# An expert's down product moved into the step of its gate and up products, with down's weights stored in one piece per partition

## The reference

```python
for gi in range(MOE_GROUPS):
    hg = jnp.einsum('td,edf->tef', t, w_gate[gi])
    hu = jnp.einsum('td,edf->tef', t, w_up[gi])
    act = jax.nn.silu(hg) * hu * gates[:, gi, :, None].astype(t.dtype)
    out = out + jnp.einsum('tef,efd->td', act, w_down[gi])
return out.reshape(b, s, d)
```

## Time and profile before

| | |
|---|---|
| median of 3 runs | 887.52 us (885.52 to 888.07) |
| the profiled execution | 885.81 us |
| its span on the core | 883.7 us |
| TensorE busy | 778.8 us, 88% |
| VectorE, ScalarE busy | 219.8 and 138.6 us |
| mean granted clock of TensorE | 0.954 of full |
| DMA | 245.29 MB, 278 GB/s over the span |

### The profile page before, as it was taken

The page is one execution under the profiler, slowest core; times in us unless marked ns, Lnnn a source line. Parts: engine busy times, 40 slices in busy tenths (PEclk is TensorE's granted clock), DMA queues, the critical chain, the costliest instruction groups (busy, mean ns, idle before and its releaser), DMA issues.

```text
span 883.7 us, 7888 instructions
## 1 busy us (share of the span) xinstructions
PE 778.8 (88%) x3080; PEld 350.3 (40%) x3080; DVE 219.8 (25%) x596; ACT 138.6 (16%) x337; POOL 29.9 (3%) x49
## 2 busy tenths in 40 slices
PE   4999977958999899989999968858999989898996
PEld 2455553553333333333445534455333323232342
DVE  0212332162124121112221452251313312121222
ACT  2013210312111010100211132122111111110031
POOL 5000000000000000000000020000000000000000
PEclk9999997969999999999999978969999999999999
DMA  8982226523999999999994070270999999999601
GB/s 249 369 299 96 95 96 263 213 94 142 383 428 418 422 423 420 421 420 406 360 199 164 0 309 1 82 299 12 365 418 424 423 418 423 418 425 415 242 1 47
DMA packets 47590, 245.29 MB, mean 278 GB/s; under 512 B 2496, under 2 KB 4768, under 8 KB 39360
## 3 DMA queue, kind: packets, MB, share of 16 engines
q1 hardware_dynamic: 45088, 240.66, 69.2%
q0 software_dynamic: 1104, 2.45, 1.0%
q10 hardware_dynamic: 1360, 1.66, 0.7%
HBM read 243.70 MB, written 1.06 MB: 277 GB/s over the span
## 4 chain that ended last, share of the span: by engine, by line
PE 67%; DMA 21%; DVE 5%; issue 4%; ACT 1%; SPq 1%; POOL 0%; ACTq 0%; POOLq 0%; DVEq 0%
DMA weights<-in_moe_w_up_dram 20%; PE bank L696 17%; PE bank L489 15%; PE bank L501 10%; PE bank L709 8%; PE bank L717 4%; PE bank L684 2%; PE bank L647 1%; PE bank L803 1%; PE bank L476 1%; PE bank L703 1%; DMA residual<-in_x_dram 1%; PE bank L537 1%; PE bank L870 1%; PE bank L861 1%
## 5 line engine op out<-in xcount | busy, mean ns | idle before, releaser
L696 PE MATMUL bank<-weights,expert_rows 128*64 128x512 f32 x1024 | 234.6, 612 | 35.1 <-DMA weights<-in_moe_w_up_dram 28.8
L696 PEld LDWEIGHTS bank<-weights,expert_rows 128*64 128x64 f32 x1024 | 84.6, 140 | 180.0 <-issue 180.0
L489 PE MATMUL bank<-weights,normalised 128*128 128x512 f32 (+1 forms) x352 | 149.9, 583 | 3.0 <-issue 3.0
L709 PE MATMUL bank<-weights,hidden_turned 128*64 128x512 f32 x512 | 116.9, 598 | 1.2 <-DVE hidden_turned L1455 0.6
L489 PEld LDWEIGHTS bank<-weights,normalised 128*128 128x128 f32 x352 | 67.1, 194 | 78.8 <-issue 77.9
L501 PE MATMUL bank<-weights,normalised 128*128 128x512 f32 x192 | 85.8, 606 | 5.6 <-ACT normalised L944 5.6
L1455 DVE COPY hidden_turned<-bank 128x256 f32<-128x256 f32 x32 | 13.6, 425 | 294.2 <-PE bank L703 294.2
L717 PE MATMUL bank<-expert_outputs,scatter_onehots 64*128 64x512 f32 x256 | 63.6, 615 | 2.4 <-ACT expert_outputs L948 2.4
L709 PEld LDWEIGHTS bank<-weights,hidden_turned 128*64 128x64 f32 x512 | 34.3, 136 | 78.8 <-issue 78.8
L501 PEld LDWEIGHTS bank<-weights,normalised 128*128 128x128 f32 x192 | 36.9, 194 | 51.5 <-issue 51.4
L1070 ACT ACTIVATE gate_tanh<-bank 128x256 f32<-128x256 f32 x32 | 12.3, 383 | 243.3 <-PE bank L696 243.3
(11 more groups left out here) (226 smaller groups left out, 507.9 us busy)
## 6 DMA issues: line engine op xcount, KB each, us to landing
weights<-in_moe_w_gate_dram SPq DMA_DIRECT2D x32, 2048.0 KB, 21.7
weights<-in_moe_w_up_dram SPq DMA_DIRECT2D x32, 2048.0 KB, 26.5
weights<-in_moe_w_down_dram SPq DMA_DIRECT2D x32, 2048.0 KB, 19.5
weights<-in_even_w_in_dram SPq DMA_DIRECT2D x6, 2048.0 KB, 17.1
weights<-in_ple_w_gate_dram SPq DMA_DIRECT2D x4, 2048.0 KB, 28.1
weights<-in_even_w_out_dram SPq DMA_DIRECT2D x2, 2048.0 KB, 18.4
weights<-in_odd_w_qkv_dram SPq DMA_DIRECT2D x2, 2048.0 KB, 19.5
weights<-in_odd_w_out_dram SPq DMA_DIRECT2D x4, 1024.0 KB, 21.5
```

The source lines that it names most:

```text
L489: mm = pe.matmul(B[bank][:, 0:width], XT[:, k, tok(t)], w[:, k, :], start=(k == 0), stop=(k == KD - 1))
L696: mm = pe.matmul(bank[j * BLK:(j + 1) * BLK, :].rearrange("p (m f) -> p m f", m=2), rows[:, k, :], W[:, slot:slot + 2, a:a + FF // 2], sta ...
L709: mm = pe.matmul(B[7][half * BLK:(half + 1) * BLK, :], ACTT[:, 2 * (f % 2) + f // 2, :], wd[:, f, half * 512:(half + 1) * 512], start=(f = ...
```

## The change

Step e of TensorE becomes: gate and up of expert e, the scatter of e-1, the transposes of e, down of e. There are 16 steps and not 17, and a down slot comes free in the step of its own gate and up. VectorE copies the turned hidden values ahead of the onehots, and ScalarE copies down's product in the same step. Down is loaded as gate and up are, rows 4p to 4p+3 in one run of 16 KB for each partition. For this each half j of the array gets other hidden columns: of every four neighbouring columns it takes two (4q+2j and 4q+2j+1), so the streamed operand of `gate_up` is read in pairs of floats, 16 bytes from pair to pair; and `turned_back` reads every second float of `US`. The counts of instructions of every kind stay as they are.

```diff
             def load(srcs, e, m, dst, done):

                 s = srcs[m][e]
-                if m < 2:
-                    sp.dma_start(dst, s.rearrange("(p k) f -> p (k f)", p=P)).then_inc(done, 16)
-                else:
-                    sp.dma_start(dst.rearrange("p (k d) -> p k d", k=KF), s.rearrange("(k p) d -> p k d", p=P))\
-                        .then_inc(done, 16)
+                sp.dma_start(dst, s.rearrange("(p k) n -> p (k n)", p=P)).then_inc(done, 16)
...
                     for k in range(KD):
                         for j in range(2):
-                            a = k * FF + j * (FF // 2)
-                            mm = pe.matmul(bank[j * BLK:(j + 1) * BLK, :].rearrange("p (m f) -> p m f", m=2), rows[:, k, :],
-                                           W[:, slot:slot + 2, a:a + FF // 2], start=(k == 0), stop=(k == KD - 1))
+                            w = W[:, slot:slot + 2, k * FF:(k + 1) * FF].rearrange("p m (q j c) -> p m q j c", j=2, c=2)
+                            mm = pe.matmul(bank[j * BLK:(j + 1) * BLK, :].rearrange("p (m q c) -> p m q c", m=2, c=2),
+                                           rows[:, k, :], w[:, :, :, j, :], start=(k == 0), stop=(k == KD - 1))
...
                     for c in range(2):
-                        mm = pe.transpose(B[6][:, c * P:(c + 1) * P], US[:, c * P:(c + 1) * P], ident)
+                        mm = pe.transpose(B[6][:, c * P:(c + 1) * P], US[:, c:2 * P:2], ident)
...
+                    gate_up(B[4 + e % 2], XE[:, e % 2], n % NSLOT).then_inc(sem("gate_up_ready"), 1)
                     if e >= 1:
-                        pe.wait_ge(sem("act_ready"), v())
-                        if v() >= 2:
-                            pe.wait_ge(sem("actt_ready"), v(-1))
-                        if e in (4, 6):
-                            pe.wait_ge(sem("pT_copied"), 2 * l + e // 2 - 1)
-                        turned_back().then_inc(sem("act_turned"), 1)
-                    if e >= 2:
-                        pe.wait_ge(sem("pt2_ready"), v(-1))
-                        pe.wait_ge(sem("ys_ready"), v(-1))
-                        scatter(e % 2, e == 2, 0)
-                        scatter(e % 2, e == 2, 1).then_inc(sem("sc_done"), 1)
-                    if e >= 1:
-                        wait_unit(u0 + 3 * (e - 1) + 2)
+                        pe.wait_ge(sem("pt2_ready"), v())
+                        pe.wait_ge(sem("ys_ready"), v())
+                        scatter((e - 1) % 2, e == 1, 0)
+                        scatter((e - 1) % 2, e == 1, 1).then_inc(sem("sc_done"), 1)
+                    pe.wait_ge(sem("act_ready"), v(1))
+                    if v() >= 1:
                         pe.wait_ge(sem("actt_ready"), v())
-                        if v() >= 2:
-                            pe.wait_ge(sem("ys_ready"), v(-1))
-                        down(unit(u0 + 3 * (e - 1) + 2).rearrange("p (k d) -> p k d", k=KF)).then_inc(sem("y_ready"), 1)
+                    if e in (4, 6):
+                        pe.wait_ge(sem("pT_copied"), 2 * l + e // 2 - 1)
+                    turned_back().then_inc(sem("act_turned"), 1)
+                    wait_unit(u0 + 3 * e + 2)
+                    pe.wait_ge(sem("actt_ready"), v(1))
+                    if v() >= 1:
+                        pe.wait_ge(sem("ys_ready"), v())
+                    down(unit(u0 + 3 * e + 2).rearrange("p (k d) -> p k d", k=KF)).then_inc(sem("y_ready"), 1)
...
-                for e in range(NE + 1):
+                for e in range(NE):
                     step(e)
```

More of the change, by code:

```diff
@@ L744, in step @@
[L744 to L754 removed]
+                    pe.wait_ge(sem("xe_ready"), v(1))
@@ L1065, in step @@
                     v = NE * l + e
-                    if e < NE:
-                        act.wait_ge(sem("gate_up_ready"), v + 1)
-                        if v >= 1:
-                            act.wait_ge(sem("ag_ready"), v)
-                        act.activation(TH, B[4 + e % 2][:, 0:256], ACT.Tanh, scale=0.5).then_inc(sem("th_ready"), 1)
+                    act.wait_ge(sem("gate_up_ready"), v + 1)
+                    if v >= 1:
+                        act.wait_ge(sem("ag_ready"), v)
+                    act.activation(TH, B[4 + e % 2][:, 0:256], ACT.Tanh, scale=0.5).then_inc(sem("th_ready"), 1)
                     if e < NE - 2:
                         rows(e + 2)
-                    if 1 <= e <= NE:
-                        act.wait_ge(sem("y_ready"), v)
-                        if e >= 3:
-                            act.wait_ge(sem("sc_done"), (NE - 1) * l + e - 2)
-                        copy(YS[:, (e - 1) % 2, :], B[7][:, :]).then_inc(sem("ys_ready"), 1)
-                for e in range(NE + 1):
+                    act.wait_ge(sem("y_ready"), v + 1)
+                    if e >= 2:
+                        act.wait_ge(sem("sc_done"), (NE - 1) * l + e - 1)
+                    copy(YS[:, e % 2, :], B[7][:, :]).then_inc(sem("ys_ready"), 1)
+                for e in range(NE):
                     step(e)
@@ L1471, in step @@
                     v = NE * l + e
-                    if 1 <= e <= NE:
-                        dve.wait_ge(sem("act_turned"), v)
-                        if v >= 2:
-                            dve.wait_ge(sem("y_ready"), v - 1)
-                        hidden_turned(sem("actt_ready"))
-                    if e < NE:
-                        gu = B[4 + e % 2]
-                        dve.wait_ge(sem("th_ready"), v + 1)
-                        dve.scalar_tensor_tensor(out=AG, in0=TH, scalar=1.0, in1=gu[:, 0:256], op0=ALU.add, op1=ALU.mult)\
-                            .then_inc(sem("ag_ready"), 1)
-                        dve.wait_ge(sem("ag_ready"), v + 1)
-                        dve.tensor_tensor(US, AG, gu[:, 256:512], ALU.mult).then_inc(sem("act_ready"), 1)
-                        if e >= 2:
-                            dve.wait_ge(sem("sc_done"), (NE - 1) * l + e - 1)
-                        onehots(e % 2, OC[:, e:e + 1], sem("first_onehots"), v + 1, sem("pt2_ready"))
+                    gu = B[4 + e % 2]
+                    dve.wait_ge(sem("th_ready"), v + 1)
+                    dve.scalar_tensor_tensor(out=AG, in0=TH, scalar=1.0, in1=gu[:, 0:256], op0=ALU.add, op1=ALU.mult)\
+                        .then_inc(sem("ag_ready"), 1)
+                    dve.wait_ge(sem("ag_ready"), v + 1)
+                    dve.tensor_tensor(US, AG, gu[:, 256:512], ALU.mult).then_inc(sem("act_ready"), 1)
+                    dve.wait_ge(sem("act_turned"), v + 1)
+                    if v >= 1:
+                        dve.wait_ge(sem("y_ready"), v)
+                    hidden_turned(sem("actt_ready"))
+                    if e >= 2:
+                        dve.wait_ge(sem("sc_done"), (NE - 1) * l + e - 1)
+                    onehots(e % 2, OC[:, e:e + 1], sem("first_onehots"), v + 1, sem("pt2_ready"))
                     if e in (3, 5):
@@ L1521, in experts @@
                 row_slots(OC2, OVW, OVO, OVR, OVO, OVR)
-                for e in range(6, NE + 1):
+                for e in range(6, NE):
                     step(e)
```

13 lines of the change are left out of this document (5 added, 8 removed).

## The result

The changed kernel takes 882.02 us in the median of 10 runs (879.4 to 885.36), the kernel before 887.17 (885.52 to 888.48). The ratio is 0.995, with a 95% interval of 0.9934 to 0.9966, so it is faster by some 5 us, where 13 had been forecast.

What follows compares the result with a forecast made beforehand. Loads pace the body and the tail is on the path regardless; 6.8 + 8.1 - 1.6 = 13.3 us, less about 0.3 for `p` weights, gives 13.0 saved: 874.5 us. Own range 869.5 to 880; the 8-in-10 range's high end 886.

Steps and rivals of the forecast that it cites:

- What bounds the kernel before: Expert stages: weight loads pace the body, one expert every 14.9 us; the tail is on the path whatever bounds the body.
- The tail: Stage end, from expert 15's gate and up to the last scatter: 14.44 us in place of 20.11.
- The scatter covers the hidden values: Before the transposes: hidden values come 1.3 us later, the scatter takes 1.92 and covers this with some 0.4 to spare.
- The step on TensorE: Body of the stages: one expert's step becomes 13.46 us, where it was 12.77, as VectorE's copy is bare.
- I take no cost: Gate and up's operand streamed in pairs: no cost taken, bounds no cost to 1.36 times the time.
- The rival of slow pairs: Every gate and up slower: 2.5 us more each at the 1.36 bound, 955 us in total; chance 0.15.
- No wait, or a small one: First product of `p` behind the stage: its weights land about when wanted, wait bounded at 0 to 1.5 us.
- the clock rival: Body: idle stretches lower TensorE's clock, 1.7 us more for a gate and up hit, total 882 to 888; chance 0.09.
- hidden values 0.3 us late in every step: Scatter not covering the hidden values in the body: 9 us lost, total 883.
- The loads: Layer 0's weight loads: down in longer runs saves 0.1 us each for 12 downs, bounds 0 and 0.2.

Runs made afterwards that it cites:

- layout_only: Kernel before with the new storage only (down in one 16 KB run, streamed pairs, transposes of every second float), old order: 881.11 us, ratio 0.9942.
- loads_only: Kernel before, old order and contiguous streams, with down in two runs of 8 KB and transposes of every second float: 881.12 us, ratio 0.9927.
- order_only: Changed kernel with streams, transposes and load of down as before the change, so the new order alone: 874.42 us, ratio 0.9859 to the kernel before.
- shifted_4: Changed kernel streaming runs of 4 floats of every 8, each moved by 2 floats across aligned 16 bytes; output not the reference's: 885.56 us, one execution.
- half_copies: New order, contiguous streams, down in two 8 KB runs, plus turned values copied in halves so down starts on the first: 875.07 us, ratio 0.9841.
- two_runs: Changed kernel with down in two runs of 8 KB, so gate and up stream contiguous halves: 874.61 us, ratio 0.9843 to the kernel before.
- runs_of_4: Changed kernel with gate and up streaming runs of 4 floats of every 8; output not the reference's: 871.54 us, one execution.

## Why the forecast failed, by its steps

**What bounds the kernel before: right.** Loads in the body, the tail on the path. layout_only and loads_only keep the old order, and their steps follow the loads (14.67 and 14.76 us).

**The tail: right.** 14.44 us forecast, 14.37 in order_only and 14.75 in the changed kernel, whose gate and up is 0.34 longer. The scatter covers the hidden values, as computed: in the first step without a scatter TensorE stood idle 1.38 us for them (1.3 forecast), in the later ones not at all.

**The step on TensorE: right for the order, wrong for the change.** 13.46 us forecast; 13.37 in order_only, 13.75 to 13.78 in the changed kernel.

**"I take no cost" for the streamed pairs: this is the step that failed.** They cost 0.34 us for each gate and up, 5%. My bounds held (nothing to 36%), but I took the lower one, and since TensorE was to pace both stages, my own threshold, "the gain of 13 us over 32 experts is gone at 0.4 us a gate and up", was nearly reached: 0.34 x 32 = 11 us. The rival of slow pairs was the right cause at the wrong size: priced from 955 us up, with 9 us or more a gate and up as its sign, it left no room for 7.34. The argument for no cost compared the time of a column (0.84 ns against 1.1 in LDWEIGHTS). The runs fit another quantity, the time for each 16 bytes touched: at full rate each matmul of a pair asks for 256 pieces in 0.44 us, 1.71 ns each, and gets them at 1.77 to 1.79. No row of the kernel before has that figure, so the forecast could not have had the cost, but it had no ground for none either. The Trainium skill, "SBUF — State Buffer", section "Door 1: The DMA port swizzle", has the same unit, a line of 16 bytes, and calls two used elements a line enough for the full rate. The line is borne out by shifted_4. The rule isn't, quite: with two floats a line for each half of the array a streamed matmul takes 612 ns against 592, gate and up 5% more, and LDWEIGHTS 206 ns against 141.

**"No wait, or a small one" behind the stage: wrong too, without effect in the changed kernel.** The prediction had the `p` stage's first product wait for the `p` projection alone, landed at 427.1. But two loads fill that slot and the product waits for both; the second, 1,024 KB of layer 1's attention weights, is issued in the kernel before at 415.38 and lands 14.6 us later, at 430.0. The prediction's own 1.5 us earlier is 428.5, 3.0 us behind the 425.5 at which it wanted the product. The changed kernel comes to the product at 434.15 and doesn't wait. order_only waits 3.87 us and half_copies 3.49.

**The account.** From the first gate and up to the last scatter, layer 0 was forecast at 422.0 - 203.74 = 218.3 us and took 430.64 - 205.38 = 225.3 in the profiled execution, 7.0 more. 16 slower products make 5.5 of it. Down of expert 0 took 5.23 us where one takes 3.65: 1.6, behind two idle stretches of 1.38 and 0.61 us, in a stretch whose mean granted clock was 0.84, so part of it at the 1.2 GHz level. The window of it, columns as above:

```profile
203.00:224.00 21.00, 16.62 (x60) 5.91 (x62) 3.09 (x7) 3.35 (x6) 0.43 (x1) 0.84 0.47 174
```

In layer 1 the sum is 835.46 - 611.81 = 223.7, 5.4 more than forecast, all of it the slower products; its down of expert 0 ran at full rate. So the clock rival did happen in this execution, once, at the start of a stage where an idle stretch is new, and never in the body. This start is where the kernels of the new order differ from one execution to another: the first step takes 16.6 and 14.9 us in the changed kernel, 16.4 and 16.3 in two_runs, 14.7 and 12.9 in order_only (608.44 to 621.37, at a granted clock of 1.00 from 606 to 622 us), where 14.6 had been forecast for both. So part of order_only's 10.8 us in layer 1 is this start.

**The number and the range.** 882.02 us lies inside the range, and by luck: that end of it came from the clock's case (882 to 888), and hidden values 0.3 us late in every step would have given 883. Neither happened in the body, where all the loss is in gate and up.

**The loads: mis-sized, without effect on the changed kernel.** Down in one run saves 0.2 us, not 0.1, still within the bounds. In the old order it shortens each step that the loads pace. In the new order it brings the `p` stage's weights earlier: they land 225.0 us behind the start of layer 0's stage in order_only (428.30) and 222.0 in runs_of_4 (426.3), which is why runs_of_4 hardly waits for them. The two halves of the change don't add: the order alone gives 12.3 us, the storage alone 5.6, both together 5.1. In the storage alone the slow pairs fit into waits for weights; in the order alone the longer step fits under the loads until expert 15. Together the waits are gone and the pairs are on the path.

**What isn't settled.** By the medians the changed kernel is 7.6 us (882.02) or, in the second series, 9.4 (883.8) behind order_only; by the spans of the profiles 10.6. In the profiles its two stages are 15.7 us longer: 28 steps of 0.41 more, two tails of 0.4 more, and 3.9 in the first steps, less 0.4 by which order_only waits for loads at expert 15. Against that order_only loses 6.4 between the stages, most of it in the wait for the `p` weights and the slow product behind it, and 0.8 behind the last; and the changed kernel's first stage started 2.1 us later in its profile. The changed kernel's own runs spread over 6 us in the first series and 10 in the second. In the kept profiles the steps of the body agree within 0.03 us for one kernel and place, while the first step of a stage takes 12.9 to 16.6 us and the first stage starts at 203.2 to 205.9; which of these makes the spread of the medians would take profiles of many executions. Open is also whether touched or shared pieces cost the time in gate and up.

## What to carry to other kernels

When a step is moved so that an engine loses its slack, every small cost on that engine that a wait used to hide comes onto the path: price the other edits of the same change again, against the new bound, and look whether the same storage can be had without them (here down in two runs of 8 KB, which leaves the streams contiguous). For a streamed float32 operand count the aligned 16-byte pieces that it touches, not the gaps: in these runs, with two halves of the array streaming together, full pieces were free in runs of 4 and of 128, half-used ones cost 5%, quarter-used ones doubled the time. And before a stage is called paced by an engine, look at what the next stage waits for, all loads on its semaphore included: there a shorter stage ran into a wait of 3.9 us. Last, before an instruction is put between two others to cover a wait, see which of them run side by side.

## What the runs showed of the hardware that was not expected

- A matmul of 512 streamed float32 columns, two of them side by side on halves of the array, takes 592 ns in the profile with 128 aligned 16-byte pieces, 611 to 612 with 256, and 1,078 with 512; pace 1.77 to 1.79 ns a piece once the pieces bind.
- Whether 256 pieces come from pairs, from single floats or from shifted runs of four makes no difference (612, 612 and 611 ns).
- LDWEIGHTS of 128 columns taken as every second float take 206 ns (207 in two_runs), every eighth float 192, contiguous 141: here a gap costs, and a wider one not more, so the count of 16-byte pieces (64, 128 and 32) doesn't give these times.
- While the stage's loads run without a break, those of 2,048 KB with 16 KB runs only reach 427 to 428 GB/s; with 8 KB runs for a third of them 425; with 4 KB runs for a third 421.
- Two scatter products of 64 rows each take as long together as one alone (1.91 us for three or for four quarters).
